# The gates' products of a visit placed between the two halves of an expert slab's products

## The reference

```
q = (xb @ w_q).reshape(128, 8, 2, 128)
s = einsum('thcd,hckd->thck', q, sub_keys)            # scores against 2 x 128 keys
s1, i1 = top_k(s[:, :, 0], 16); s2, i2 = top_k(s[:, :, 1], 16)
top_s, pos = top_k(all sums of a s1 and a s2, 16)     # 16 of 256 candidates, per head
eidx = the expert (0..16383) of each
gate = softmax(top_s)
h = gelu(einsum('thkd,td->thk', u[eidx], xb))
y = einsum('thk,thkd->td', gate * h, v[eidx])
```

## Time and profile before

| | us |
|---|---|
| median of 3 runs | 2211.22 |
| the profiled execution | 2210.88 |
| its span, first to last instruction | 2209.1 |
| visits 23 to 61, first and second layer | 250.80 and 250.84 |

### The profile page before, as it was taken

The page is one execution under the profiler, slowest core; times in us unless marked ns, Lnnn a source line. Parts: engine busy times, 40 slices in busy tenths (PEclk is TensorE's granted clock), DMA queues, the critical chain, the costliest instruction groups (busy, mean ns, idle before and its releaser), DMA issues.

```text
span 2209.1 us, 38524 instructions
## 1 busy us (share of the span) xinstructions
PE 2186.6 (99%) x12830; PEld 1915.6 (87%) x12830; DVE 1548.6 (70%) x3175; ACT 1213.4 (55%) x1831; POOL 1115.3 (50%) x491
## 2 busy tenths in 40 slices
PE   9999999999999999999999999999999999999998
PEld 7998989998888888888888889888888888888886
DVE  5623844435997888877777765499788887777777
ACT  5545645444568777744333346455777775333333
POOL 7978259586888777730000025678877774000000
PEclk9999999999999999999999999999999999999999
DMA  7645436356555544465566554545554445665653
GB/s 248 235 157 183 153 130 219 115 186 205 170 188 180 168 163 162 163 207 193 195 193 210 193 177 144 179 165 191 181 171 164 162 163 200 194 195 191 212 195 126
DMA packets 109930, 398.98 MB, mean 181 GB/s; under 512 B 12784, under 2 KB 13168, under 8 KB 109040
## 3 DMA queue, kind: packets, MB, share of 16 engines
q1 hardware_dynamic: 104832, 380.16, 51.9%
q10 hardware_dynamic: 4976, 17.17, 2.4%
HBM read 394.13 MB, written 3.15 MB: 180 GB/s over the span
## 4 chain that ended last, share of the span: by engine, by line
PE 92%; DVE 5%; issue 2%; ACT 1%; POOL 1%; DVEq 0%; ACTq 0%; POOLq 0%
PE GG L639 22%; PE GG L647 11%; PE XX L474 11%; PE XX L475 11%; PE XX L476 11%; PE GG L474 6%; PE GG L476 6%; PE GG L475 6%; PE XX L963 1%; PE XX L965 1%; PE GG L541 1%; PE GG L528 1%; DVE hT_both L2388 1%; PE GG L534 1%; DVE hot L2331 1%
## 5 line engine op out<-in xcount | busy, mean ns | idle before, releaser
L2544 POOL TENSOR_TENSOR w_lo<-ring,w_hi 128x1024 fp32r<-128x1024 f32 (+1 forms) x464 | 1104.9, 2405 | 735.2 <-ACT w_hi L1188 731.6
L1188 ACT ACTIVATE w_hi<-ring 128x1024 fp32r<-128x1024 f32 x722 | 757.7, 1057 | 731.2 <-PE XX L476 393.3
L639 PE MATMUL GG<-hT_both,w_hi 128*128 128x512 f32 x2208 | 534.7, 394 | 0.0
L639 PEld LDWEIGHTS GG<-hT_both,w_hi 128*128 128x128 f32 x2208 | 404.7, 188 | 78.9
L474 PE MATMUL XX<-w_hi,hT_both 128*128 128x512 f32 x1024 | 398.8, 389 | 1.8 <-DVE w_lo L2405 1.1
L475 PE MATMUL XX<-w_lo,hT_both 128*128 128x512 f32 x1024 | 398.4, 389 | 0.0
L476 PE MATMUL XX<-w_hi,hT_both 128*128 128x512 f32 x1024 | 398.4, 389 | 0.0
L2405 DVE TENSOR_TENSOR w_lo<-ring,w_hi 128x1024 fp32r<-128x1024 f32 x248 | 303.9, 1225 | 56.0 <-ACT w_hi L1188 55.9
L647 PEld LDWEIGHTS GG<-hT_both,w_lo 128*128 128x128 f32 x2208 | 283.4, 191 | 10.9
L647 PE MATMUL GG<-hT_both,w_lo 128*128 128x256 f32 x2208 | 286.4, 282 | 0.0
L474 PEld LDWEIGHTS XX<-w_hi,hT_both 128*128 128x128 f32 x1024 | 192.2, 188 | 43.2 <-DVE w_lo L2405 2.3
(11 more groups left out here) (329 smaller groups left out, 2788.0 us busy)
## 6 DMA issues: line engine op xcount, KB each, us to landing
ring<-slabs_in SPq DMA_DIRECT2D x722, 512.0 KB, 3.9
big<-rows_in ACTq DMA_DIRECT2D x10, 512.0 KB, 6.6
big<-rows_in ACTq DMA_DIRECT2D x3, 1024.0 KB, 6.4
big<-keys_in ACTq DMA_DIRECT2D x2, 1024.0 KB, 8.6
h_kept<-h ACTq DMA_DIRECT2D x2, 1024.0 KB, 12.2
h<-h_kept ACTq DMA_DIRECT2D x2, 1024.0 KB, 5.1
big<-ws_in ACTq DMA_DIRECT2D x1, 1024.0 KB, 8.0
out<-h SPq DMA_DIRECT2D x4, 256.0 KB, 2.0
```

The source lines that it names most:

```text
L639: last = nc.tensor.matmul(GG[pair][:, a, :], w_hi[:, 2 * (s % 2) + half, w], hT_both[:, c, :, :].rearrange("p s t -> p (s t)"), start=c == ...
L1188: nc.scalar.activation(w_hi[:, 2 * j + half, 0:n], ring[j][:, half * 1024:half * 1024 + n], ACT.Copy).then_inc(hi_ready, 1)
L2544: Q.tensor_tensor(w_lo[:, 2 * j + half, 0:n], ring[j][:, half * 1024:half * 1024 + n], w_hi[:, 2 * j + half, 0:n], ALU.subtract).then_inc( ...
```

## The change

On TensorE, the gates of a visit are issued inside `project_merged`, through a function `between`, behind the products with `w_hi` and ahead of those with `w_lo`. On ScalarE, a visit's order becomes: `copy_part`, split of half 0, `hot1` of the groups x + 3, GELU, split of half 1. On VectorE: for each group `times_gates`, `hot2`, `hot1`; then the sum and `times_gelu`. No operation is added or removed.

```
-            def project_merged(l, m):
+            def project_merged(l, m, between=lambda: None):
...
                 rounded_weights(1)
+                between()
                 if m < QUERIES + 63:
                     rest_of_weights(0)
                 rest_of_weights(1)
...
                 for n in range(GATED - 1, 64):
-                    project_merged(l, QUERIES + n)
-                    for x in groups_of(n) if GATED <= n < GATED + SPAN else []:
-                        gates(x)
+                    project_merged(l, QUERIES + n, lambda: [gates(x) for x in groups_of(n) if GATED <= n < GATED + SPAN])
...
                 for n in range(GATED, GATED + SPAN):
+                    copy_part(QUERIES + n)
                     split_half(SLAB0[f"u{l}"] + n + RING, 0)
-                    copy_part(QUERIES + n)
-                    split_half(SLAB0[f"u{l}"] + n + RING, 1)
-                    gelu_in_place(n, n)
                     for x in groups_of(n):
                         if x + 3 < GROUPS:
                             hot1(x + 3)
+                    gelu_in_place(n, n)
+                    split_half(SLAB0[f"u{l}"] + n + RING, 1)
...
                 for n in range(GATED, GATED + SPAN):
-                    sum_parts(QUERIES + n)
-                    for i, x in enumerate(groups_of(n)):
+                    for x in groups_of(n):
                         times_gates(x)
                         if x + 2 < GROUPS:
                             hot2(x + 2)
-                        if i == 0:
-                            times_gelu(n)
-                    for x in groups_of(n):
                         hot1(x + 3)
+                    sum_parts(QUERIES + n)
+                    times_gelu(n)
```

## The result

The changed kernel takes 2222.2 us (median of 5 runs, 2222.11 to 2223.61) against 2211.33 us before (2211.07 to 2212.7): a ratio of 1.005, with a 95% interval of 1.0039 to 1.0061, so some 10.9 us slower. The forecast was 2221, from 2211 to 2231. The profiled execution took 2223.61 us, with a span of 2221.8.

A forecast was written before the change was run, and what follows sets the result against it. TensorE, busy 2186.6 of 2209.1 us, was taken as the bound. Per stage 7.2 us of new waits less 2.45 of old ones made +9.5 us over two stages; on 2211.22 that gave 2221 us, range 2211 to 2231.

The forecast's parts named there:

- The bound and the ceiling: TensorE, visits 23 to 61: products take 248.4 us of 250.8; waits of 2.45 us a stage are the most to win.
- The old waits: TensorE's gates waiting for VectorE's hot1, six times 0.5 us, would end; gain 4.9 us with the rest of the waits.
- The step from gates to the products of 256 columns: TensorE: new step replaces gates to 512-column products; taken at 0.08 us a visit, bounds 0 to 0.19, net nothing.
- The estimate of 0.05: Same TensorE step from the skill's weight-load figure and the gates' pace: 0.05 us, making the forecast 2.3 us lower.
- The late GELU: ScalarE: GELU behind two hot1 frees the pair of banks at E + 6.70; TensorE waits 0.62 or 0.17 us.
- E: Moment on TensorE when a visit's 256-column products are issued and the next visit's 512-column products follow.
- The knock-on: After visits 29, 40, 51, VectorE's list starts late; banks free 7.28 us behind, against 6.08: three waits of 1.20 us.
- The sum: Per stage 7.2 us of new waits less 2.45 of old ones, +4.76; two stages +9.5 us.
- The covers: split_half of half 1, its GpSimd rest and slab loads end later but hidden, with 1.6 us or more: cost nothing.
- The other rivals: Cover holds, 2206.3 us, chance 0.12; waits in part, 2215.9, chance 0.11; VectorE not catching up, 2239, chance 0.07.
- the cover holds: Rival: ScalarE starts the GELU by E + 4.68, so only the gain is left, 2206.3 us; chance 0.12.
- VectorE caught up: Rival said it would not: every two-group visit waits 0.66 us, 16.5 us a stage, 2239 us; chance 0.07.

The follow-up runs named there:

- gelu_between2: Changed kernel with ScalarE's GELU between a visit's two hot1, placed by the group's position in the visit: 2206.15 us against 2211.24 for the kernel before, ratio 0.9976.
- vector_old: Changed kernel with VectorE's order of the kernel before put back: 2352.99 us, one timed execution.
- gates_only: Kernel before with TensorE's part of the change alone, ScalarE and VectorE keeping their old orders: 2314.78 us, one timed execution.
- scalar_old: Changed kernel with ScalarE's order of the kernel before put back: 2246.57 us against 2212.25 for the kernel before, ratio 1.016.
- longer_hot1: Changed kernel with two small unused operations ahead of each hot1 on ScalarE from group 3 on: 2239.34 us against 2212.25 for the kernel before, ratio 1.0125.
- gates_behind: Changed kernel with only TensorE's order put back, gates behind the products of 256 columns: 2239.69 us against 2211.24 for the kernel before, ratio 1.013.

## Why the prediction was right

**The bound and the ceiling.** TensorE's own products were put at 248.4 us a stage and the waits at 2.45. Gelu_between2 measures 248.29 with no wait left: the ceiling was right.

**The old waits go.** They did: no gates wait in the changed kernel.

**The step from gates to the products of 256 columns** was taken at 0.08 us with bounds from 0 to 0.19. It is 0.08 to 0.09 (2.00 against 1.91). The estimate of 0.05 worked out from the figure of the Trainium skill (TensorE: Matmul & The Clock Gate, LDWEIGHTS) was too low, as the load of 187 to 192 ns in the earlier trace rows had suggested.

**The late GELU.** Forecast against the trace of visit 27: GELU at E + 5.30, measured 5.32 (733.76 - 728.44); to `times_gelu` 0.61, measured 0.61; to TensorE 0.79, measured 0.74 (735.11 - 734.37). Free at E + 6.70, measured 6.67.

**The knock-on.** From one late release to the next 7.28 us were forecast behind visit 29; measured 755.67 - 748.41 = 7.26. The visits named (29, 31, 32, and so on) and their number, 11 a stage, were those of the trace.

**What was mis-sized.** The sum had 9.5 us; the stages grew by 11.0. The term that was too small is the wait itself: I let TensorE go on at full pace behind it, with 0.1 us on each wait only in the range. But a block of line 639 that has waited, with the two groups of gates behind it, takes 739.75 - 735.11 = 4.64 us, against 746.28 - 741.75 = 4.53 for an undisturbed one. That is some 0.1 us on each of 11 waits; over the first stage, block by block, it is 1.3 us. The waits themselves were shorter than forecast (1.06 for 1.20 behind visit 31, 3.06 less 2.00; 0.58 for 0.62 behind visit 28, 2.58 less 2.00), 6.6 us a stage in place of 7.2. A last 0.2 us stands in three blocks that the next paragraph tells of. 248.29 us without any wait (gelu_between2) + 6.6 + 1.3 + 0.2 make 256.4, and the stage has 256.32. So two errors of opposite sign stand in the sum, and that it came so near owes something to luck; the visits and the number of the waits do not.

**The covers.** `split_half` of half 1, its rest on GpSimd and the loads were costed at nothing, and no wait on weights showed up in the stage. The other rivals fell too: the cover of the rival "the cover holds" wasn't there, and VectorE caught up, so that visits 33 and 34 do not wait. It took longer than the visit or two that were forecast. In visit 33 its list starts at 767.62 = E - 1.21 (E is 768.83), behind the `times_gelu` of visit 32, where E - 2.05 was reckoned with; `times_gelu` starts at 774.15, and the block of visit 35 begins at 774.91 = E + 6.08. So the 0.8 us of cover in a two-group visit were just used up there, and two more times like it; the blocks of visits 35, 46 and 57 take 0.05 to 0.07 us longer.

## What to carry to other kernels

When an engine's list is rearranged so that one consumer gets its data earlier, work out for each result that another engine waits for how many instructions now stand ahead of it, and hold that against the length of one round; here 3.7 us of `hot1` ahead of a 0.6 us GELU were 0.6 us too many. An engine at 76% busy can still set the end: what counts is its place in the list at the moment when its result is wanted. A change whose gain is real but covered by a new wait is worth one more edit: moving one instruction of the list turned 11 us lost into 5 us won.

## What the runs showed of the hardware

A wait of TensorE costs more than its length: the block behind it takes about 0.1 us longer, as above. Its weight loads fit that. In the changed kernel, the first load of the undisturbed block at 728.44 starts 0.12 us ahead of the block's first product, beside the products before; behind the wait, load and product both start at 735.11. That this is the reason was not tested.

```profile
728.32 3.51 PEld L639 LDWEIGHTS GG<-hT_both,w_hi 128*128 128x128 f32 x16
...
735.11 3.50 PEld L639 LDWEIGHTS GG<-hT_both,w_hi 128*128 128x128 f32 x16 [0.64 <-DVE big L2350]
```

The long waits of vector_old cost more still. TensorE waited for 2.71 us ahead of one group of gates, and in the stretch behind it the granted clock was below its full level:

```profile
728.25 0.25 PE L964 MATMUL XX<-hot 128*128 128x128 f16 x1 [2.71 <-DVE hot L2330]
...
729.00 3.35 PE L647 MATMUL GG<-hT_both,w_lo 128*128 128x256 f32 x16
732.19 1.08 PE L639 MATMUL GG<-hT_both,w_hi 128*128 128x512 f32 x4
```

```profile
720.90:729.00 8.10, 5.17 (x34) 4.06 (x33) 6.59 (x13) 4.80 (x9) 5.43 (x3) 0.96 0.44 152
729.00:732.20 3.20, 3.20 (x20) 3.20 (x18) 0.00 (x0) 0.00 (x0) 0.00 (x0) 0.58 0.55 169
732.20:736.10 3.90, 3.79 (x18) 2.81 (x16) 2.95 (x6) 3.68 (x9) 2.08 (x1) 1.00 0.00 0
```

The block of line 647 takes 732.19 - 729.00 = 3.19 us in place of 2.00, at a mean granted clock of 0.58, nearly the lower of the two levels (1.2 GHz of 2.4). Over both stages the clock was 0.93 in vector_old and 0.94 in gates_only, while it was 1.00 from 1030 to 1600 us, between the stages, in both; so it is no trait of these two executions as a whole. In scalar_old, with waits of up to 2.1 us in TensorE's own row, it was 0.99 and 0.98 in the two stages. In the changed kernel, whose waits in that row are at most 0.9 us, it stayed at 1.00, and so it did in longer_hot1 and gates_behind with waits of up to 1.3 and 1.2 us.

This is why vector_old and gates_only came out slower than the waits alone had made them: the expectation had reckoned with the full clock. In vector_old TensorE stood idle for 47 us of the stage (321.82 less 274.56 of busy time), fewer than the 58 expected (306 less 248.4), but the same products kept it busy for 26 us more than in gelu_between2 (274.56 against 248.29). At the full clock, the 20 waits a stage of gates_behind add 4.5 us to the busy time (252.83). By that an estimate for the 29 waits of vector_old is some 7 of the 26 us, which leaves some 19 to the lower clock.
